# Last down projection with tokens in rows over the transposed residual in PSUM, a norm per token, matmuls of ones at the beginning, and another order of VectorE's work

## The chip, the cores and the metric

One core of one Trainium2 chip runs the whole program. The metric is device time in microseconds (us): the median of three runs of the kernel before is 1358.28 us (1357.35 to 1358.91). A profile of one execution goes with it, and its own time is given below.

## What is computed

Two blocks of two layers each, on 256 tokens of 1024 features, in fp32. Every layer is a mixer (differential attention, neighbourhood attention, convolution and pooling, forgetting and block attention), a feed-forward part of 2816 hidden features, and in the first block a gated extra. Each part reads an RMS norm of the residual `h` and adds to `h`. The end, which the change rewrites, is this:

```python
def rmsnorm_2(x, g):
    xf = x.astype(jnp.float32)
    y = xf * lax.rsqrt(jnp.mean(xf * xf, axis=-1, keepdims=True) + RMS_EPS)
    return (y * g.astype(jnp.float32)).astype(x.dtype)

def conv_ffn(h, w_in, conv_w, conv_b, w_out):
    z = h @ w_in
    u, g = z[..., :D_FF], z[..., D_FF:]
    a = causal_dwconv(u, conv_w) + conv_b
    return (jax.nn.silu(a) * g) @ w_out
...
        h = h + conv_ffn(rmsnorm_2(h, ffn_norm_g[layer]), ffn_w_in[layer],
                         ffn_conv_w[layer], ffn_conv_b[layer], ffn_w_out[layer])
    return rmsnorm_2(h, final_norm_g)
```

## The kernel before

**Layout.** The residual `h` lies in SBUF with features on the partitions: 8 tiles of 128 features by 256 tokens. Every product is made of three fp32r products, since each operand is split in two parts: a weight chunk `raw` of 1 MB is rounded by ScalarE to `whi` (its `split`, L647), VectorE subtracts to get `wlo` (its `split`, L990), and `x`, `hid` and the rest have a high and a low part too. TensorE multiplies high by high, high by low and low by high.

**The ring.** Weights pass through a ring of three chunks (`RING`), in the order of `PLAN`: v, qk, wo, ffn, down, and so on for each layer. SyncE starts the load of chunk c when VectorE has made `wlo` of chunk c-3 (`w_lo`); ScalarE casts it when TensorE is through with chunk c-3 (`w_used`); TensorE starts a chunk at `w_lo`. No scheduler orders anything: each engine's program is written out by hand in the block of that engine, and runs strictly in that order, so an instruction that waits holds back all that stands behind it.

**Attention** (`attention(a)`, a = 0, 1, 2) runs in steps s = 0 to 23, two for each pair of heads j = (s-4)//2. In each step TensorE runs a tile of the qk or wo projection, and between its halves one small product of the attention: scores (L1755), transposes of the probabilities (L1779), probabilities times v (`times_v`, L1795 for a = 0, L1808 else), and for a = 0 transposes of the normalised output (`o_transposes`, L1817). In even steps VectorE adds the bias and takes the maximum (`bias_max`, L1152 or L1158, L1168) and ScalarE takes exponentials (`exps`, L740). In odd steps VectorE normalises (`normalise`, L1185 to L1207), splits a weight chunk, and either scales the output (`norm_o`, L1217, for a = 0; it waits for GpSimd's power L563) or makes its low part (`lo_out`, L1229; `lo_out` of a = 0 is L1225, in even steps). ScalarE copies the transposed probabilities (`take_T`, L753), squares the output (`square_o`, L759) and casts it (`take_o`, L769, L773).

**Norms.** Feature-major `h` makes a norm a chain over all engines: ScalarE squares (L693), GpSimd adds (L499 to L512), TensorE sums over partitions with ones (`sum_squares`, L1524), VectorE adds epsilon (`means`, L1027), GpSimd takes the power -0.5 (L520, five more operations for "mix2", L524 to L529), VectorE builds a diagonal (`diagonals`, L1036), TensorE spreads it (`spread_r`, L1534), VectorE copies it (`take_r`, L1045). Where TensorE does its two parts within other work is set by `SUM_AT` and `SPREAD_AT` for the v projections, and by `middle` for the feed-forward.

**After a wo projection** VectorE adds each pair of feature tiles to `h` (`update`, L1059), ScalarE and VectorE make the next `x` (`take_x` L675, `lo_x` L1016), and VectorE then splits the next two chunks. **Feed-forward** chunks are looped three at a time; VectorE's split of the chunk three ahead stands behind the product of the current chunk with the norm.

**The last stage**: `down(3, "final")` runs 12 chunks (kind "D", 256 output features by 8, 8 or 6 hidden tiles) with the weights stationary: per hidden tile and 128 output features a matmul of 512 columns and one of 256 (`two`, L1546 to L1549). Four times VectorE adds the result to `h` (L1347, L1348), ScalarE squares and scales by gamma (`final_scale`, L878), and after the last pair the whole norm chain follows, then four products (L1504) and four stores (L467) of the feature-major output. The neighbourhood bias `nab` (3 MB) is loaded by GpSimd's queue in two transfers right after the norm of ffn0 (`load_neighbourhood`, L555).

## Time and profile before

| | us |
|---|---|
| median of three runs | 1358.28 |
| the profiled execution's own time | 1354.73 |
| its span, first to last instruction | 1352.7 |
| TensorE busy (matmuls) | 1270.6 |
| VectorE busy | 942.0 |
| ScalarE busy | 678.6 |
| GpSimd busy | 168.9 |
| mean granted TensorE clock | 0.983 |

The profiled execution is 3.6 us shorter than the median. Its time lies 2.0 us over its span. TensorE's clock has two levels in this trace, 1.0 (2.4 GHz) and 0.5 (1.2 GHz). Stages by time: v0 8 to 39 us, attention 0 to 160, ffn0 166 to 299, down0 to 360, gate0 to 390, v1 to 415, attention 1 to 514, ffn1 520 to 648, down1 to 710, gate1 to 740, the input projection "ev" of the convolution and pooling mixer to 798, its output projection "evout" to 824, ffn2 to 956, down2 to 1019, v3 to 1042, attention 2 to 1145, ffn3 to 1277, down3 to 1339, and the end to 1352.7. A matmul row's duration includes its way through the array, so that rows overlap; the pace of a stream is the distance of the starts. fp32 products (both operands fp32) show two records each.

### The profile page before, as it was taken

How to read it: one execution, taken by the hardware profiler on the slowest of the kernel's cores; microseconds unless marked ns; L12 is line 12 of the kernel's file. 1: busy time of each engine (PE TensorE's matmuls, PEld its weight loads, DVE VectorE, ACT ScalarE, POOL GpSimd, SP SyncE). 2: the span in 40 equal slices, each digit the busy share in tenths (PEclk: the TensorE clock that was granted, in tenths of full speed). 3: DMA queues.
4: the chain of work that ended last, by engine and by line, in shares of the span. 5: the costliest groups of instructions: out<-in, count | busy, mean ns of one | idle time of the engine just before them, and what ended most of it. 6: DMA issues, size and time to landing. Idle time of an engine off the chain costs nothing.

```text
span 1352.7 us, 22276 instructions
## 1 busy us (share of the span) xinstructions
PE 1270.6 (94%) x8682; PEld 1158.9 (86%) x8682; DVE 942.0 (70%) x1215; ACT 678.6 (50%) x975; POOL 168.9 (12%) x157
## 2 busy tenths in 40 slices
PE   6987899999999889999999899999999999999996
PEld 5876787888988778888889889999888888999985
DVE  4855668778577665877657794887857765787753
ACT  4544435554455655555445334655435655555541
POOL 3000120016120002000011622000312000100001
PEclk9988899999999999999999999999999999999998
DMA  7422398655646234765564455976465524676550
GB/s 274 147 72 94 94 213 229 186 179 183 201 141 215 94 94 133 218 186 178 181 201 156 150 186 146 271 199 184 150 202 158 162 94 125 177 197 183 174 172 31
DMA packets 286134, 224.22 MB, mean 166 GB/s; under 512 B 8216, under 2 KB 276544, under 8 KB 285936
## 3 DMA queue, kind: packets, MB, share of 16 engines
q1 hardware_dynamic: 283888, 214.25, 52.4%
q0 software_dynamic: 2176, 8.99, 2.5%
q8 instruction: 50, 0.82, 0.3%
q14 instruction: 20, 0.16, 0.0%
HBM read 222.15 MB, written 2.63 MB: 166 GB/s over the span
## 4 chain that ended last, share of the span: by engine, by line
PE 70%; DVE 18%; ACT 5%; issue 3%; DMA 2%; POOL 1%; SPq 0%; POOLq 0%; DVEq 0%; ACTq 0%
PE ps L1548 20%; PE ps L1549 10%; PE ps L1539 10%; PE ps L1540 10%; PE ps L1541 10%; DVE wlo L990 6%; PE ps L1547 2%; DVE x L1016 2%; ACT prob L740 1%; ACT whi L647 1%; PE ps L1755 1%; DMA raw<-in_ffn_w_up 1%; PE ps L1672 1%; DVE nmax L1168 1%; PE ps L1674 1%
## 5 line engine op out<-in xcount | busy, mean ns | idle before, releaser
L990 DVE TENSOR_TENSOR wlo<-raw,whi 128x2048 fp32r<-128x2048 f32 (+1 forms) x206 | 471.8, 2294 | 135.4 <-ACT whi L647 134.4
L647 ACT CAST whi<-raw 128x2048 fp32r<-128x2048 f32 (+1 forms) x206 | 385.2, 1873 | 225.9 <-PE ps L1541 136.6
L1539 PE MATMUL ps<-x,whi 128*128 128x256 f32 (+1 forms) x1640 | 478.5, 292 | 18.5 <-DVE wlo L990 6.4
L1540 PE MATMUL ps<-x,whi 128*128 128x256 f32 (+1 forms) x1640 | 467.7, 285 | 0.0
L1541 PE MATMUL ps<-x,wlo 128*128 128x256 f32 (+1 forms) x1640 | 467.2, 285 | 0.0
L1539 PEld LDWEIGHTS ps<-x,whi 128*128 128x128 f32 (+1 forms) x1640 | 317.7, 194 | 28.5 <-issue 11.2
L1540 PEld LDWEIGHTS ps<-x,whi 128*128 128x128 f32 (+1 forms) x1640 | 318.2, 194 | 0.5
L1541 PEld LDWEIGHTS ps<-x,wlo 128*128 128x128 f32 (+1 forms) x1640 | 317.6, 194 | 0.0
L1548 PE MATMUL ps<-hid,whi 128*128 128x512 f32 x672 | 236.6, 395 | 1.1 <-DVE hid L1274 1.1
L1548 PE MATMUL ps<-x,whi 128*128 128x512 f32 x616 | 222.9, 401 | 8.3 <-DVE wlo L990 8.3
L1549 PE MATMUL ps<-hid,wlo 128*128 128x256 f32 x672 | 188.4, 280 | 0.0
L1549 PE MATMUL ps<-x,wlo 128*128 128x256 f32 x616 | 173.3, 281 | 0.0
L1548 PEld LDWEIGHTS ps<-hid,whi 128*128 128x128 f32 x672 | 126.0, 188 | 29.4 <-DVE hid L1274 1.4
L1548 PEld LDWEIGHTS ps<-x,whi 128*128 128x128 f32 x616 | 116.5, 189 | 34.2 <-DVE wlo L990 6.7
L1549 PEld LDWEIGHTS ps<-hid,wlo 128*128 128x128 f32 x672 | 126.9, 189 | 1.4
L499 POOL TENSOR_TENSOR ssum<-ssum,sq 128x512 f32<-128x512 f32 x24 | 36.2, 1510 | 710.7 <-ACT sq L693 710.7
L1549 PEld LDWEIGHTS ps<-x,wlo 128*128 128x128 f32 x616 | 117.0, 190 | 3.5
L846 ACT COPY gu<-ps 128x512 f32<-128x512 f32 x44 | 25.7, 584 | 85.7 <-PE ps L1547 85.7
L675 ACT ACTIVATE x<-h,gcol 128x256 fp32r<-128x256 f32 x72 | 32.6, 501 | 66.3 <-DVE h L1348 45.7
L740 ACT ACTIVATE prob<-prob,nmax 128x256 f32<-128x256 f32 (+1 forms) x96 | 46.3, 483 | 28.8 <-DVE nmax L1168 25.1
L1016 DVE SCALAR_TENSOR_TENSOR x<-h,gcol,x 128x256 fp32r<-128x256 f32 x72 | 38.7, 580 | 20.9 <-ACT x L675 20.9
L1326 DVE TENSOR_TENSOR gu<-ps,gu 128x512 f32<-128x512 f32 x44 | 30.3, 690 | 27.3 <-ACT gu L846 27.2
(177 smaller groups left out, 1294.2 us busy)
## 6 DMA issues: line engine op xcount, KB each, us to landing
raw<-in_ffn_w_in SPq DMA_DIRECT2D x88, 512.0 KB, 5.1
raw<-in_ffn_w_gate SPq DMA_DIRECT2D x44, 512.0 KB, 4.1
raw<-in_ffn_w_up SPq DMA_DIRECT2D x44, 512.0 KB, 5.2
raw<-in_ffn_w_down SPq DMA_DIRECT2D x32, 512.0 KB, 4.1
raw<-in_ffn_w_out SPq DMA_DIRECT2D x32, 512.0 KB, 4.5
raw<-in_da_w_qkv SPq DMA_DIRECT2D x24, 512.0 KB, 4.6
raw<-in_na_w_qkv SPq DMA_DIRECT2D x24, 512.0 KB, 4.5
raw<-in_od_w_in SPq DMA_DIRECT2D x24, 512.0 KB, 4.6
```

The source lines that it names most:

```text
L499: nc.gpsimd.tensor_tensor(total, total, more, ALU.add).then_inc(add_ok, 1)
L647: nc.scalar.copy(whi[:, c % RING, 0:n], raw[:, c % RING, 0:n]).then_inc(w_hi, 1)
L675: nc.scalar.activation(xs[XBUF[name]][:, k, 0, :], h[:, k, :], ACT.Copy, scale=gamma(name, k)).then_inc(x_hi, 1)
L740: ins = nc.scalar.activation(prob[:, u % 4, off:off + n], prob[:, u % 4, off:off + n], ACT.Exp, bias=nmax[:, u, t:t + 1], accum_out=sums[: ...
L990: nc.vector.tensor_tensor(wlo[:, c % RING, 0:n], raw[:, c % RING, 0:n], whi[:, c % RING, 0:n].bitcast(F32), ALU.subtract).then_inc(w_lo, 1)
L1016: nc.vector.scalar_tensor_tensor(out=x[:, k, 1, :], in0=h[:, k, :], scalar=gamma(name, k), in1=x[:, k, 0, :].bitcast(F32), op0=ALU.mult, o ...
L1326: nc.vector.tensor_tensor(g, ps[:, b0:b0 + 2, 0:S], g, ALU.add).then_inc(sum_ok, 1)
L1539: mm(dst, hi, x[:, 0, :], start=start, stop=False)
L1540: mm(dst, hi, x[:, 1, :], start=False, stop=False)
L1541: return mm(dst, lo, x[:, 0, :], start=False, stop=stop)
L1548: mm(dst, hi, x.rearrange("p a t -> p (a t)"), start=start, stop=False)
L1549: return mm(dst[:, 0:S], lo, x[:, 0, :], start=False, stop=False)
```

## The change

The host now gets the output as tokens by features, and gamma of the last norm goes in as a row of its own. The parts, in the order of the program:

1. TensorE begins with 14 fp32 products of `ones` by `ones` into a bank that is overwritten later.
2. Attention 0: ScalarE's `take_T(j-1)` moves from the odd step into the even step before it, between the two `exps`. VectorE's odd step becomes split, `normalise` twice, `norm_o`.
3. Attention 1 and 2: VectorE's odd step becomes `normalise` twice, `lo_out`, split.
4. `updates`: `update(p+1)` stands ahead of `lo_x(p)`, in wo0, wo1, wo3 and evout.
5. Feed-forward: `spread_r` stands ahead of chunk 2 instead of in its middle.
6. `nab` is loaded in eight pieces of two heads, each after two more chunks of ffn0.
7. `SUM_AT` of v1 moves by 12 matmuls, from (1, 1) to (2, 0).
8. "mix2": the first two chunks of "ev" are gone through in feature tiles 0 to 3, 4 to 5, 6 to 7 instead of 0 to 5, 6 to 7; VectorE splits the chunk `START["ev"] + RING` between `means` and `diagonals`.
9. "ev": `pool_lo` stands ahead of the convolution.
10. down3: 16 fp32 products with the identity put the transposed `h` into banks 0 to 3, and 11 chunks (kind "T", two hidden tiles by 1024 output features) are added to it with `hid` stationary, 24 matmuls of 512 columns each. Bank 2t + n holds tokens 128t and on, features 512n and on. ScalarE squares each bank with a sum per token, VectorE adds epsilon, GpSimd takes the power, VectorE multiplies by gamma and by the power, and SyncE stores four times 256 KB.

```diff
     start, at = {}, 0
     for name, kind, n in plan:
...
 SS = 4
-SUM_AT = {"v0": (2, 0), "v1": (1, 1), "v3": (1, 1)}
+SUM_AT = {"v0": (2, 0), "v1": (2, 0), "v3": (1, 1)}
...
+            for q in (0, 1, 3, 2):
+                if q == 2:
+                    sp.wait_ge(out_ac, 1)
+                else:
+                    sp.wait_ge(out_ok, (1, 2, 0, 3)[q])
+                t, n = q // 2, q % 2
+                sp.dma_start(out[t * P:(t + 1) * P, n * 512:(n + 1) * 512], y_part(q)
+                             ).then_inc(store, 16)
...
+                    for piece in range(HEADS // 2):
+                        gp.wait_ge(w_used, START["ffn0"] + 4 + 2 * piece)
+                        load_neighbourhood(2 * piece)
+                    gp.wait_ge(nab_in, 16 * HEADS)
...
+            gp.wait_ge(w_used, START["ffn3"])
+            gp.dma_start(gfin, w["gfin"].partition_broadcast(P)).then_inc(gfin_in, 16)
+            for t in range(TT):
+                gp.wait_ge(fmean_ok, t + 1)
+                nc.gpsimd.tensor_tensor(final_rstd(t), fsum[:, 4 + t:5 + t], half[:, 0:1], ALU.pow
+                                        ).then_inc(frstd_ok, 1)
...
                             exps(2 * j)
+                        if a == 0 and 0 <= j - 1 < PAIRS:
+                            take_T(j - 1)
+                        if 0 <= j < PAIRS:
                             exps(2 * j + 1)
                     else:
                         if a and 0 <= j - 1 < PAIRS:
                             take_o(j - 1)
                         if a == 0 and 0 <= j - 1 < PAIRS:
-                            take_T(j - 1)
                             square_o(j - 1)
                         if a and 0 <= j < PAIRS:
...
+                for q in range(4):
+                    if q < 3:
+                        ac.wait_ge(part_out, FOURTH["down3"] + q + 1)
+                    else:
+                        ac.wait_ge(w_used, last("down3") + 1)
+                    nc.scalar.activation(fsq(q), bank(q), ACT.Square, scale=D ** -0.5,
+                                         accum_out=fsum[:, q:q + 1]).then_inc(fsq_ok, 1)
+                ac.wait_ge(frstd_ok, 2)
+                ac.wait_ge(fhg_ok, 3)
+                nc.scalar.activation(y_part(2), hg_part(2), ACT.Copy, scale=final_rstd(1)
+                                     ).then_inc(out_ac, 1)
...
+            def updates(wname, banks, name):
+
+                update(wname, banks, name, 0)
+                for p in range(4):
+                    if p < 3:
+                        update(wname, banks, name, p + 1)
+                    lo_x(name, p)
+                split(last(wname) - 1 + RING)
+                split(last(wname) + RING)
...
+                    if a and 0 <= j < PAIRS:
+                        normalise(2 * j)
+                        normalise(2 * j + 1)
+                    if a and 0 <= j - 1 < PAIRS:
+                        lo_out(j - 1)
+                    if 3 <= s < STEPS - 1:
+                        split(START[qk] + s // 2 - 1 + RING)
+                    if a == 0 and 0 <= j < PAIRS:
+                        normalise(2 * j)
+                        normalise(2 * j + 1)
                     if a == 0 and 0 <= j - 1 < PAIRS:
                         norm_o(j - 1)
-                    if a and 0 <= j - 1 < PAIRS:
-                        lo_out(j - 1)
-                    if 0 <= j < PAIRS:
-                        normalise(2 * j)
-                        if a == 0:
-                            normalise(2 * j + 1)
-                    if 3 <= s < STEPS - 1:
-                        split(START[qk] + s // 2 - 1 + RING)
-                    if a and 0 <= j < PAIRS:
-                        normalise(2 * j + 1)
...
             means("mix2")
+            split(START["ev"] + RING)
             diagonals("mix2")
...
             for i in range(6):
                 copy_out(i)
-                split(START["ev"] + i + RING)
+                if i:
+                    split(START["ev"] + i + RING)
                 if i in (1, 2):
                     final_first(4 * (i - 1))
 
+            pool_lo(0)
+            pool_lo(2)
...
             split(START["ev"] + 6 + RING)
-            pool_lo(0)
-            pool_lo(2)
...
+            splits("down3")
+
+            def final_mean(t):
+                ve.wait_ge(fsq_ok, 2 * t + 2)
+                nc.vector.tensor_scalar(fsum[:, 4 + t:5 + t], fsum[:, 2 * t:2 * t + 1],
+                                        fsum[:, 2 * t + 1:2 * t + 2], NORM_EPS, ALU.add, ALU.add
+                                        ).then_inc(fmean_ok, 1)
+
+            def final_gamma(q):
+                ve.wait_ge(fsq_ok, q + 1)
+                n = q % 2
+                nc.vector.tensor_tensor(hg_part(q), bank(q), gfin[:, n * 512:(n + 1) * 512],
+                                        ALU.mult).then_inc(fhg_ok, 1)
+
+            def final_scale(q):
+                ve.wait_ge(frstd_ok, q // 2 + 1)
+                ve.wait_ge(fhg_ok, q + 1)
+                nc.vector.tensor_scalar(y_part(q), hg_part(q), final_rstd(q // 2), None, ALU.mult
                                         ).then_inc(out_ok, 1)
+
+            ve.wait_ge(gfin_in, 16)
+            final_gamma(0)
+            final_mean(0)
+            final_gamma(1)
+            final_scale(0)
+            final_scale(1)
+            final_gamma(2)
+            final_mean(1)
+            final_gamma(3)
+            final_scale(3)
...
                 x = xs[XBUF[name]]
-                for k0, k1 in ((0, 6), (6, KT)):
+                for k0, k1 in ((0, 4), (4, 6), (6, KT)):
...
-                    if first and jj:
-                        middle = lambda: (sum_squares if jj == 1 else spread_r)(name)
+                    if first and jj == 1:
+                        middle = lambda: sum_squares(name)
+                    if first and jj == 2:
+                        spread_r(name)
...
+                    pe.wait_ge(w_lo, c + 1)
+                    pe.wait_ge(hid_lo, 3 * FT + 2 * i + 2)
+
+                    def piece(kk, t, n):
+                        f = 2 * i + kk
+                        ts, cs = slice(t * P, (t + 1) * P), slice(n * 512, (n + 1) * 512)
+                        dst, end = bank(2 * t + n), f == FT - 1
+                        mm(dst, hid[:, f, 0, ts], hi[:, kk, cs], start=False, stop=False)
+                        mm(dst, hid[:, f, 0, ts], lo[:, kk, cs], start=False, stop=False)
+                        return mm(dst, hid[:, f, 1, ts], hi[:, kk, cs], start=False, stop=end)
+
+                    if i < n_chunks - 1:
+                        for kk in range(2):
+                            for t in range(TT):
+                                for n in range(2):
+                                    ins = piece(kk, t, n)
+                        ins.then_inc(w_used, 1)
+                        continue
+                    for t in range(TT):
+                        for n in range(2):
+                            for kk in range(2):
+                                ins = piece(kk, t, n)
+                            ins.then_inc(w_used if t == 1 and n == 1 else part_out, 1)
...
 
+            pe.wait_ge(ones_ok, 1)
+            for _ in range(14):
+                mm(bank(0)[:, 0:P], ones[:], ones[:], start=True, stop=True)
             for layer in range(2):
                 mix, ple, gate = f"mix{layer}", f"ple{layer}", f"gate{layer}"
...
-            down(3, "final")
-            sum_squares("final")
-            spread_r("final")
+            for k in range(KT):
+                for t in range(TT):
+                    mm(bank(2 * t + k // 4)[:, (k % 4) * P:(k % 4 + 1) * P],
+                       h[:, k, t * P:(t + 1) * P], ident, start=k % 4 == 0, stop=False)
+            down_t()
 
```

What this makes of VectorE's order in one pair of heads of attention 0 (L1152/L1190 is `bias_max`, L1217/L1255 `norm_o`, L1225/L1263 `lo_out`, L990/L1018 the split; the first number of each is the line before, the second after). Before:

```order
L1217 TENSOR_SCALAR onrm<-ps,ostat 128x128 x2
L1185 RECIPROCAL rsum<-sums 128x2 x2
L1189 TENSOR_SCALAR rsum<-rsum,tiny 128x2
L1194 TENSOR_SCALAR prob<-prob,rsum 128x256 x2
L1200 SCALAR_TENSOR_TENSOR prob<-prob,rsum 128x256 x2
L990 TENSOR_TENSOR wlo<-raw,whi 128x2048
L1152 SCALAR_TENSOR_TENSOR prob<-dist,ps 128x512
L1168 TENSOR_REDUCE nmax<-prob 128x2
L1152 SCALAR_TENSOR_TENSOR prob<-dist,ps 128x512
L1168 TENSOR_REDUCE nmax<-prob 128x2
L1225 SCALAR_TENSOR_TENSOR x<-ps,col,x 128x256
```

And of the same engine at the same place now:

```order
L1018 TENSOR_TENSOR wlo<-raw,whi 128x2048
L1223 RECIPROCAL rsum<-sums 128x2 x2
L1227 TENSOR_SCALAR rsum<-rsum,tiny 128x2
L1232 TENSOR_SCALAR prob<-prob,rsum 128x256 x2
L1238 SCALAR_TENSOR_TENSOR prob<-prob,rsum 128x256 x2
L1255 TENSOR_SCALAR onrm<-ps,ostat 128x128 x2
L1190 SCALAR_TENSOR_TENSOR prob<-dist,ps 128x512
L1206 TENSOR_REDUCE nmax<-prob 128x2
L1190 SCALAR_TENSOR_TENSOR prob<-dist,ps 128x512
L1206 TENSOR_REDUCE nmax<-prob 128x2
L1263 SCALAR_TENSOR_TENSOR x<-ps,col,x 128x256
```

The split has moved from the end of the odd step to its beginning, and `norm_o` from the beginning to the end.

ScalarE in the same pair of heads, before (L740 `exps`, L753 `take_T`, L759 `square_o`, L769 `take_o`):

```order
L769 ACTIVATE x<-ps,col 128x256
L740 ACTIVATE prob,sums<-prob,nmax 128x256 x4
L753 COPY probT<-ps 128x512
L759 ACTIVATE osq,ostat<-ps 128x128 x2
L728 ACTIVATE qkT<-ps 128x512
L647 CAST whi<-raw 128x2048
```

ScalarE there now:

```order
L796 ACTIVATE x<-ps,col 128x256
L767 ACTIVATE prob,sums<-prob,nmax 128x256 x2
L780 COPY probT<-ps 128x512
L767 ACTIVATE prob,sums<-prob,nmax 128x256 x2
L786 ACTIVATE osq,ostat<-ps 128x128 x2
L755 ACTIVATE qkT<-ps 128x512
L674 CAST whi<-raw 128x2048
```

The copy of the transposed probabilities has moved between the exponentials of the two heads.

VectorE at the norm "mix2", before the change (L1026 and L1027 are `means`, L1036 `diagonals`, L1091 `copy_out`):

```order
L1026 COPY tiny<-ps 128x2
L1027 TENSOR_SCALAR tiny<-ps 128x2
L1036 TENSOR_TENSOR sq<-cst,tiny 128x256 x2
L1409 COPY ya<-ps 128x256
L1410 COPY rst<-ps 128x256
L1091 TENSOR_TENSOR pool<-ps,rst 128x2x256
L990 TENSOR_TENSOR wlo<-raw,whi 128x2048
```

VectorE there now:

```order
L1054 COPY tiny<-ps 128x2
L1055 TENSOR_SCALAR tiny<-ps 128x2
L1018 TENSOR_TENSOR wlo<-raw,whi 128x2048
L1064 TENSOR_TENSOR sq<-cst,tiny 128x256 x2
L1443 COPY ya<-ps 128x256
L1444 COPY rst<-ps 128x256
L1129 TENSOR_TENSOR pool<-ps,rst 128x2x256 x2
```

The split has moved ahead of the diagonals, into the time in which GpSimd works on the powers.

## Rows read from the trace of the kernel before

**Rows 1.** Waits of TensorE: line, waited-for engine and line: total us, times, longest

```profile
PE ps L1795 <- ACT probT L753: 17.4, 7, 3.3
PE ps L1524 <- POOL ssum L512: 9.7, 3, 3.8
PE ps L1779 <- DVE prob L1207: 9.1, 15, 0.9
...
PE ps L1548 <- DVE wlo L990: 8.3, 5, 2.9
PE ps L1539 <- DVE wlo L990: 6.4, 5, 2.6
PE ps L1539 <- DVE x L1016: 3.5, 2, 3.1
...
PE ps L1539 <- DVE x L1417: 2.5, 1, 2.5
...
PE ps L1539 <- DVE x L1225: 2.2, 1, 2.2
```

**Rows 2.** Busy time by stretch: us, then each engine's busy us, granted clock, DMA

```profile
82.04:85.45 3.41, 3.41 (x19) 3.19 (x17) 0.77 (x4) 0.62 (x4) 0.88 (x2) 0.50 0.00 0
93.84:105.95 12.11, 8.76 (x71) 8.05 (x71) 7.73 (x15) 6.14 (x16) 0.88 (x2) 1.00 0.25 87
...
216.00:296.00 80.00, 80.00 (x456) 69.57 (x455) 62.27 (x73) 43.30 (x59) 0.00 (x0) 1.00 0.67 191
```

**Rows 3.** VectorE's timeline in attention 0: start, duration, group, idle before and releaser

```profile
96.75 0.61 DVE L1217 TENSOR_SCALAR onrm<-ps,ostat 128x128 f32<-128x128 f32 x2 [4.17 <-POOL ostat L563]
...
99.38 2.28 DVE L990 TENSOR_TENSOR wlo<-raw,whi 128x2048 fp32r<-128x2048 f32 x1
```

**Rows 4.** ScalarE's timeline in the same pair of heads

```profile
105.33 0.56 ACT L753 COPY probT<-ps 128x512 f32<-128x512 f32 x1
```

**Rows 5.** VectorE's timeline in attention 1

```profile
471.89 0.42 DVE L1229 TENSOR_TENSOR x<-ps,x 128x256 fp32r<-128x256 f32 x1 [1.42 <-ACT x L773]
```

**Rows 6.** TensorE's timeline in ffn0, at two places

```profile
186.65 0.51 PE L1548 MATMUL ps<-x,whi 128*128 128x512 f32 x1 [1.39 <-DVE wlo L990]
...
206.77 0.50 PE L1548 MATMUL ps<-x,whi 128*128 128x512 f32 x1 [2.92 <-DVE wlo L990]
```

**Rows 7.** DMA issues: target and source, queue, count, size of each, us to landing

```profile
nab<-in_rpb POOLq DMA_DIRECT2D x2, 1536.0 KB, 16.9
```

**Rows 8.** GpSimd's timeline: the power at v1, and the first power at "mix2"

```profile
402.69 2.68 POOL L520 TENSOR_TENSOR tiny<-tiny,half 128x2 f32<-128x2 f32 x1 [2.59 <-DVE tiny L1027]
...
757.88 0.70 POOL L524 TENSOR_TENSOR tiny<-tiny,half 128x2 f32<-128x2 f32 x1 [3.47 <-DVE tiny L1027]
```

**Rows 9.** VectorE's timeline at v1: the split beside that power

```profile
402.52 2.28 DVE L990 TENSOR_TENSOR wlo<-raw,whi 128x2048 fp32r<-128x2048 f32 x1
```

**Rows 10.** TensorE's timeline: one `times_v` and what follows; v0; down3's first and last

```profile
93.84 1.16 PE L1795 MATMUL ps<-v,probT 128*128 128x128 f32 x8 [2.16 <-ACT probT L753]
94.76 0.36 PE L1539 MATMUL ps<-x,whi 128*128 128x256 f32 x1
...
17.17 0.39 PE L1672 MATMUL ps<-whi,x 128*128 128x512 f32 x1
...
21.70 0.39 PE L1674 MATMUL ps<-whi,x 128*128 128x512 f32 x1
...
1277.06 0.40 PE L1548 MATMUL ps<-hid,whi 128*128 128x512 f32 x1
...
1338.71 0.40 PE L1547 MATMUL ps<-hid,whi 128*128 128x512 f32 x1
```

**Rows 11.** Timeline of the end, VectorE and SyncE's queue

```profile
1339.15 0.69 DVE L1347 TENSOR_TENSOR h<-ps,h 128x512 f32<-128x512 f32 x1 [9.26 <-PE ps L1547]
...
1347.17 2.50 DVE L1504 TENSOR_TENSOR spare<-spare,rst 128x512 f32<-128x512 f32 x4
1347.88 2.18 SPq L467 DMA_DIRECT2D out<-spare  x4
```

112 lines of the change are left out of this document (46 added, 66 removed).

## The prediction

> **What bounds the kernel now.** I read the page first: TensorE is busy 94% of the span, so time is won only where it waits, where its clock is low, or where it does less. Then the table of what it waits for [rows 1]. Its large lines are each one pattern that comes back: the copy of the transposed probabilities in attention 0 (17.4 us, 7 times), the sums of GpSimd (9.7 us, 3 times), VectorE's normalisation in attention 1 and 2 (9.1 us, 15 times), and weights not yet split (8.3 and 6.4 us). Then the clock. The table by stretches shows 0.5 for 3.41 us after a wait of 2.73 us, with TensorE busy throughout, and 1.00 in an 80 us stretch without a wait [rows 2]; the clock's record has eleven such stretches of 3.41 us besides the start, all beside waits of about 2 us or more, five of them in attention 0. In such a stretch half the work is done, so each costs up to 1.7 us. A wait that goes can thus give back more than itself.
>
> **Attention 0.** A pair of heads takes 12.1 us, in which TensorE is busy 8.8 us and VectorE 7.7 [rows 2]. VectorE first waits 4.17 us for GpSimd's power, then normalises and only then splits, so that the split ends at 101.7 us [rows 3] and delays the maxima, then both exponentials, and behind them the copy `take_T` at 105.33 [rows 4], for which TensorE waits. In the new order the split fills the time of that wait, and `take_T` goes ahead of the second head's exponentials. I worked one pair of odd j through, with TensorE never waiting and its pair beginning at 0: scores end at 1.1, maxima at 3.8, transposes of the pair before at 4.8, `take_T` at 5.4, `times_v` wants it at 6.3. The second exponentials end at 6.6, the split too, `normalise` at 8.8, `norm_o` at 9.6, and TensorE wants that at 11.3. For the next (even) j scores end at 11.3, and `norm_o` at 19.6 where TensorE wants it at 20.1: the slack there is 0.5 us. So TensorE sets the pace, at 8.8 us. That takes all 17.4 us, and of the five low-clock stretches about 1.6 each, 7.9 together: 25.3. VectorE's 7.7 to 8.2 us a pair are near TensorE's 8.8, and GpSimd's powers now fall beside `normalise`; I leave 1.0 for that. At the end of the attention the split no longer stands between `norm_o` and `lo_out`: of the 2.2 us [rows 1] 1.1 go, as the cast and `lo_out` remain; the low-clock stretch behind it goes with an even chance (0.8), and wo0's wait for its second ffn chunk, 0.8, by `updates`. Sum: -25.3 +1.0 -1.1 -0.8 -0.8 = -27.0. The other end is VectorE as the bound with 10.5 us a pair.
>
> **Attention 1 and 2.** `normalise` of the first head waited behind `lo_out`, itself idle 1.42 us for ScalarE's cast [rows 5], though its exponentials were done. Its turn comes 1 us earlier; transposes wait no more, -9.1 [rows 1]. The later `lo_out` and split are wanted only a step or more later.
>
> **updates.** One `update` ahead saves VectorE about 1.7 us on the way to the next x and to its split. The waits for wlo behind wo1 and wo3, 1.8 and 1.7 us, go (both are in [rows 1]'s 8.3 and 6.4). Behind evout ScalarE's cast is late as well; of 2.6 us I take 1.4, and 1.2 for the low clock that follows it now. Sum: -6.1.
>
> **spread_r ahead of chunk 2.** The norm arrives 3 us earlier and the split behind it too. The four waits for it (1.39 us in ffn0 [rows 6], as much in ffn1, 0.58 in ffn2 and ffn3) go: -3.9. VectorE's diagonals are ready 1.2 us before the new place.
>
> **nab in eight pieces.** The two transfers of 1.5 MB took 16.9 us [rows 7] beside the weights, and TensorE waited 2.92 us [rows 6], with a low-clock stretch behind it. A piece is 0.4 MB per two chunks, 12 us, in a ring that has some 7 us to spare. -2.9 -1.6 = -4.5.
>
> **v1.** The 2.23 us before the sums are within the 9.7 [rows 1]. The sums move 12 matmuls later, but VectorE begins `means` only behind a split that ends at 402.5, and GpSimd's power then takes 2.68 us beside the next split [rows 8, 9]. So diagonals are done at 405.8 as before, and TensorE, 2.2 us ahead, waits there. -0.3; the bounds are 0 and -2.2.
>
> **mix2.** The first chunk waited for x of tiles 4 and 5 (3.1 and 0.5 us, the 3.5 of [rows 1]); the second chunk's four tiles now fill that, and the sums come when GpSimd has them, 2.1 us earlier. But the split moves beside GpSimd's chain of six operations. At v1 the same neighbourhood stretched one power to 2.68 us where it takes 0.70 alone [rows 8], with the split running [rows 9]. I take that: the chain ends 2.1 us later than it would, which eats the gain, and TensorE waits some 4 us for the diagonals, long enough for a low clock: +0.8. Without stretching it would be -2.4. The Trainium skill (SBUF — State Buffer, "Who interferes with whom") says that a VectorE instruction with two SBUF inputs and a GpSimd instruction that reads SBUF shut each other out for the whole instruction, the first to issue going first. By that rule the move to this place is a mistake worth the whole 2.1 us; were there no such lock, the total below would be 3.2 us less. The trace agrees with it at v1, and the operand that matters, two SBUF inputs, is that of the split.
>
> **ev.** `pool_lo` moves ahead of work of 8 us that it does not need; its 2.5 us [rows 1] go, and what is put behind it is wanted 3 us or more later. -2.5.
>
> **down3.** Before, 176 pairs of a 512 and a 256 column matmul from 1277.06 to 1339.06, 0.352 us each [rows 10]. Now 264 matmuls of 512 columns with data as stationary side, the form of v0, where 20 take 4.53 us, 0.2265 each [rows 10]: 59.8, or -2.2. The 16 fp32 products with the identity cost what the four of `times_v` do, 0.92 us for four at full clock [rows 10]: +3.7. Nothing hides them, as hid is ready. Sum +1.5. A chunk lasts 5.4 us and needs 1.9 of ScalarE and 2.3 of VectorE: the ring holds. Bounds: 0 and +6.
>
> **The end.** 13.6 us from the last matmul to the span's end [rows 11]. Now: Square of one bank with its sum 0.75 (an estimate: 0.63 for the Square of 512 columns now and 0.1 for reading the sum), mean 0.2, power 0.75, scale 0.6: the last operand is ready 2.5 us after the last matmul, the second store is issued at about 3.3, and the end lay 2.6 us behind the last issue: 5.8. The other three banks are done by then or beside it. -7.8, between -7.0 and -9.0.
>
> **The beginning.** 14 fp32 products at low clock end near 7 us, before the first weights at 8.4, so they delay nothing. The first 12 matmuls then run at full clock, 2.4 us sooner, but TensorE must wait until 25.7 for GpSimd's sums (3.6 us now, in [rows 1]), 1.3 us longer, and the low clock that follows that wait costs as much or more: +0.5, between -1.6 and +1.7.
>
> **The sum.** -27.0 -9.1 -6.1 -3.9 -4.5 -0.3 +0.8 -2.5 +1.5 -7.8 +0.5 = -58.4 us. From the profiled execution's 1354.7 that is 1296.3; it was 3.6 us below the median, so I take the same off the median: 1358.3 - 58.4 = 1299.9 us.
>
> **The rivals.** (a) VectorE binds attention 0. With 8.2 us of own work, links between dependent steps and locks against GpSimd, a pair takes 10.5 instead of 8.8. For it speaks the slack of 0.5 us; against it, that VectorE's order has idle time only once per two pairs and still fits. Seven pairs by 1.7: 1311.8 us. (b) The freed waits turn up as waits for weights: with denser work the ring's load, cast and split are late in attention 0 and in down3. For it speaks that wlo is the second releaser now; against it, 191 GB/s in the 80 us without a wait [rows 2], more than down3 needs. At 1 us for each of 11 chunks, 1310.9. (c) Better: mix2 is not stretched, v1 and evout give their whole waits, no low clock after attention 0: 1299.9 - 3.2 - 1.9 - 1.2 - 0.8 = 1292.8. (d) The change does not do what it says: attention 0 keeps its waits because another copy or power comes last; only the rest comes, 1299.9 + 25 = 1325. (e) Slower: a clock that denser work does not keep. All of some 1260 us of matmul work would have to run at a mean of 0.955 instead of nearly 1 to eat 58 us; at 0.93 it is 1299.9 + 95 = 1395. Against it: 1.00 over the 80 us without any wait [rows 2].
>
> **How the numbers follow.** Forecast, 1296 to 1306: 0.53. (c) 0.14. (a) 0.13. (b) 0.09. (d) 0.09. (e) 0.01, and 0.01 for something unseen. The range takes the forecast, (c), (a) and (b): 1290 to 1317. A difference of 0.2%, 2.7 us, is what can be told from no change: faster 0.98, same 0.01, slower 0.01.
>
> **What would show it.** In the changed profile, the row of `times_v` waiting for probT should be gone or under 3 us, pairs 8.8 us apart, and no low clock between 66 and 150 us. L1779's waits gone; no wait of 2.9 us in ffn0; GpSimd's first power at mix2 near 2.7 us instead of 0.70, and a new wait for the diagonals there of about 4 us; one of 2 us at v1's diagonals. Down3 from ffn3's end to the last matmul 63.5 us; the end 5.8 us. I am wrong if pairs of attention 0 take over 10 us, or down3 over 66.

## The result and the profile after

The changed kernel takes 1296.0 us (median of four runs, 1295.85 to 1298.22), beside 1358.6 us (1357.35 to 1359.62) for the kernel before: a ratio of 0.9543, 95% interval 0.9527 to 0.956. The forecast was 1299.9 us, with a range of 1290 to 1317, and 58.4 us less than before; the medians lie 62.6 us apart, the two profiled executions 56.3 (spans of 1352.7 and 1296.4). The second is a difference of two single executions: that of before was 3.9 us below its median, that of after 2.2 above. On three other chips the kernel before had medians of 1355.4 to 1356.1, and the changed one, run again, 1296.64, which is 59 us apart. So the sum was about right in size, but it was right by terms that missed in both directions, as the comparison by stage shows.

What TensorE waits for in the changed kernel, to be read beside [rows 1] (line, engine and line waited for, total us, times, longest):

```profile
PE ps L1590 <- DVE wlo L1018: 5.4, 4, 1.7
PE ps L1575 <- POOL ssum L531: 5.0, 2, 4.5
PE ps L1723 <- DVE wlo L1025: 2.9, 1, 2.9
PE ps L1599 <- DVE wlo L1018: 2.6, 2, 1.3
PE ps L1585 <- DVE sq L1064: 2.5, 1, 2.5
PE ps L1575 <- DVE wlo L1018: 1.9, 1, 1.9
```

The 17.4 us for the transposed probabilities and VectorE's 9.1 us of the normalisation are gone. Two rows stand for new waits: `spread_r` at mix2 waits 2.5 us for the diagonals (L1585, 0.86 us before), and v1's sums wait 1.9 us for weights (L1575, where 2.23 us for GpSimd's sums stood). The second ffn chunk waits 1.3 us at each of its four places (in L1590 and L1599), where 0.80, 1.79, 2.58 and 1.69 us stood at wo0, wo1, evout and wo3. The 4.5 us of L1575 are v0's sums, 3.62 us before.

Busy time by stretch (us from:to, length, then the busy us of TensorE, its weight loads, VectorE, ScalarE and GpSimd with counts, the granted clock, DMA share and GB/s), to be read beside [rows 2]:

```profile
93.43:101.97 8.54, 8.54 (x73) 8.03 (x72) 8.33 (x16) 6.25 (x18) 0.92 (x2) 1.00 0.35 125
25.12:31.95 6.83, 5.56 (x15) 4.62 (x16) 2.81 (x3) 2.66 (x2) 4.12 (x5) 0.50 0.41 134
56.00:132.00 76.00, 73.60 (x601) 68.77 (x599) 63.67 (x121) 49.26 (x128) 7.59 (x16) 1.00 0.46 141
369.86:373.27 3.41, 3.41 (x10) 2.74 (x10) 2.36 (x3) 0.89 (x1) 2.72 (x2) 0.50 0.75 247
721.43:724.84 3.41, 3.41 (x14) 3.06 (x14) 1.70 (x4) 0.00 (x0) 1.53 (x3) 0.50 1.00 326
```

One pair of heads of attention 0 (first row) takes 8.54 us instead of 12.11, with TensorE busy in all of it. The clock is full through the attention (third row). It is low in three places only, besides the start and the last microseconds: around the sums of v0 (from 25.12 us, within the wait for them), behind the sums of v1, and behind the new wait at mix2.

Where the 56.3 us come from, by stage. Each length is the distance between the first records of two events that both traces have (a norm's sums, its `spread_r`, the first product with hid; for the end of ffn3 of the changed kernel the first product with the identity):

| stretch | before | after | difference | forecast |
|---|---|---|---|---|
| start to `spread_r` of v0 | 33.31 | 34.99 | +1.7 | +0.5 |
| to ffn0's sums (attention 0) | 142.48 | 113.86 | -28.6 | -27.0 |
| to the end of ffn0 | 122.78 | 116.42 | -6.4 | -5.9 |
| down0, gate0, v1 to its `spread_r` | 107.67 | 109.16 | +1.5 | -0.3 |
| attention 1 to ffn1's sums | 123.87 | 116.52 | -7.4 | with attention 2: -12.6 |
| ffn1 | 118.14 | 116.41 | -1.7 | -1.4 |
| down1, gate1 to its `spread_r` | 73.62 | 73.39 | -0.2 | 0 |
| ev, evout to ffn2's sums | 114.72 | 111.02 | -3.7 | -4.3 |
| ffn2 | 119.78 | 119.23 | -0.6 | -0.6 |
| down2, v3 | 76.87 | 77.32 | +0.5 | 0 |
| attention 2 to ffn3's sums | 124.05 | 120.27 | -3.8 | see above |
| ffn3 | 119.77 | 118.94 | -0.8 | -0.6 |
| down3 and the end | 75.68 | 68.90 | -6.8 | -6.3 |

(The forecast's terms are put where they fall; `updates` is split over the stretches of its four places.)

The lengths before are those of one execution. Other traces below have the same code in some of these stretches, and two stretches scatter widely: attention 0 takes 142.5, 140.3 and 141.3 us in the three traces that have its old code, and ffn0 takes 120.8 to 124.3 us in six. Measured against these, attention 0 gains 26.4 to 28.6 us and not one sharp number.

The last stage, to be read beside [rows 10] and [rows 11] (timeline: start, duration, engine, line, group, idle before and releaser):

```profile
1227.53 3.74 PE L2024 MATMUL ps<-cst,h 128*128 128x128 f32 x32
1231.02 0.47 PE L1803 MATMUL ps<-whi,hid 128*128 128x512 f32 x1
...
1290.61 3.54 SPq L486 DMA_DIRECT2D out<-spare  x4
1290.76 0.39 PE L1805 MATMUL ps<-whi,hid 128*128 128x512 f32 x1
...
1291.18 0.60 ACT L902 ACTIVATE spare<-ps 128x512 f32<-128x512 f32 x1 [0.67 <-PE ps L1805]
1291.68 0.19 ACT L902 ACTIVATION_READ_ACCUMULATOR spare<-ps 128x1 f32 x1
...
1292.20 0.55 POOL L652 TENSOR_TENSOR fsum<-fsum,half 128x1 f32<-128x1 f32 x1 [2.13 <-DVE fsum L1531]
1292.79 0.72 ACT L906 ACTIVATE spare<-spare,fsum 128x512 f32<-128x512 f32 x1 [0.91 <-POOL fsum L652]
```

The 16 products with the identity (two records each) take 3.5 us until the first real one, where 3.7 were forecast. The last matmul starts at 1290.76, and from its end at 1291.15 the chain Square, sum, mean, power, scale, store takes 5.3 us to the end of the span, where 5.8 were forecast and 13.6 were needed before.

### The profile page after: what moved, and what is told of

Its sections match the earlier page's. It is cut to its first block, busy times and chain, and to the rows that moved or that the text cites. A ratio compares the mean times of both kernels' runs of the same rounds, so it can differ in the third digit from the quotient of the medians.

```text
span 1296.4 us, 22210 instructions
## 1 busy us (share of the span) xinstructions
PE 1260.0 (97%) x8648; PEld 1149.5 (89%) x8648; DVE 943.4 (73%) x1208; ACT 675.2 (52%) x971; POOL 170.3 (13%) x168
## 4 chain that ended last, share of the span: by engine, by line
PE 84%; DVE 9%; ACT 2%; DMA 2%; issue 1%; POOL 1%; SPq 1%; POOLq 0%; ACTq 0%
PE ps L1599 19%; PE ps L1590 13%; PE ps L1591 12%; PE ps L1592 12%; PE ps L1600 10%; DVE wlo L1018 3%; DVE x L1044 3%; PE ps L1598 2%; PE ps L1838 2%; ACT whi L674 2%; PE ps L1803 1%; PE ps L1805 1%; PE ps L1804 1%; PE ps L1862 1%; PE ps L1723 1%; PE ps L1891 1%
## 5 line engine op out<-in xcount | busy, mean ns | idle before, releaser
L1018 DVE TENSOR_TENSOR wlo<-raw,whi 128x2048 fp32r<-128x2048 f32 (+1 forms) x205 | 467.9, 2286 | 134.9 <-ACT whi L674 134.0
L1590 PE MATMUL ps<-x,whi 128*128 128x256 f32 (+1 forms) x1640 | 474.7, 289 | 11.2 <-DVE wlo L1018 5.4
L1590 PEld LDWEIGHTS ps<-x,whi 128*128 128x128 f32 (+1 forms) x1640 | 313.8, 191 | 21.3 <-issue 9.3
L1591 PEld LDWEIGHTS ps<-x,whi 128*128 128x128 f32 (+1 forms) x1640 | 314.1, 192 | 0.5
L1592 PEld LDWEIGHTS ps<-x,wlo 128*128 128x128 f32 (+1 forms) x1640 | 313.8, 191 | 0.0
L1599 PE MATMUL ps<-x,whi 128*128 128x512 f32 x616 | 222.2, 399 | 2.6 <-DVE wlo L1018 2.6
L1599 PE MATMUL ps<-hid,whi 128*128 128x512 f32 x504 | 177.7, 395 | 1.1 <-DVE hid L1312 1.1
L1600 PE MATMUL ps<-hid,wlo 128*128 128x256 f32 x504 | 141.3, 280 | 0.0
L1599 PEld LDWEIGHTS ps<-x,whi 128*128 128x128 f32 x616 | 115.9, 188 | 28.4 <-issue 3.2
L1599 PEld LDWEIGHTS ps<-hid,whi 128*128 128x128 f32 x504 | 94.5, 188 | 22.5 <-DVE hid L1312 1.4
L518 POOL TENSOR_TENSOR ssum<-ssum,sq 128x512 f32<-128x512 f32 x22 | 34.2, 1558 | 524.4 <-ACT sq L720 523.9
L1600 PEld LDWEIGHTS ps<-hid,wlo 128*128 128x128 f32 x504 | 95.2, 189 | 1.0
L1044 DVE SCALAR_TENSOR_TENSOR x<-h,gcol,x 128x256 fp32r<-128x256 f32 x72 | 48.1, 714 | 11.1 <-ACT x L702 11.1
L1364 DVE TENSOR_TENSOR gu<-ps,gu 128x512 f32<-128x512 f32 x44 | 30.4, 691 | 30.5 <-ACT gu L875 30.4
```

The lines of the kernel that those rows point to most:

```text
L518: nc.gpsimd.tensor_tensor(total, total, more, ALU.add).then_inc(add_ok, 1)
L1018: nc.vector.tensor_tensor(wlo[:, c % RING, 0:n], raw[:, c % RING, 0:n], whi[:, c % RING, 0:n].bitcast(F32), ALU.subtract).then_inc(w_lo, 1)
L1044: nc.vector.scalar_tensor_tensor(out=x[:, k, 1, :], in0=h[:, k, :], scalar=gamma(name, k), in1=x[:, k, 0, :].bitcast(F32), op0=ALU.mult, o ...
L1364: nc.vector.tensor_tensor(g, ps[:, b0:b0 + 2, 0:S], g, ALU.add).then_inc(sum_ok, 1)
L1590: mm(dst, hi, x[:, 0, :], start=start, stop=False)
L1591: mm(dst, hi, x[:, 1, :], start=False, stop=False)
```

## The experiments

There were twelve more runs: eleven other kernels, and the changed kernel again. They come from three chips, so each median is given with its ratio to the kernel before on the same chip, and the stage lengths of the traces are used where less than 2 us is at stake. Most stages that the code leaves alone come out within 0.1 us of each other between traces. Where a low clock falls in one and not in the other, or a load comes later, they differ by up to 3.5 us, so a stage length says little unless the clock in it is compared too.

### Attention 0: which of the two edits

Both edits alone, upon the kernel before:

```diff
                             exps(2 * j)
+                        if a == 0 and 0 <= j - 1 < PAIRS:
+                            take_T(j - 1)
+                        if 0 <= j < PAIRS:
                             exps(2 * j + 1)
...
                         if a == 0 and 0 <= j - 1 < PAIRS:
-                            take_T(j - 1)
                             square_o(j - 1)
...
-                    if a == 0 and 0 <= j - 1 < PAIRS:
-                        norm_o(j - 1)
+                    if a == 0 and 3 <= s < STEPS - 1:
+                        split(START[qk] + s // 2 - 1 + RING)
                     if a and 0 <= j - 1 < PAIRS:
                         lo_out(j - 1)
                     if 0 <= j < PAIRS:
                         normalise(2 * j)
                         if a == 0:
                             normalise(2 * j + 1)
-                    if 3 <= s < STEPS - 1:
+                    if a == 0 and 0 <= j - 1 < PAIRS:
+                        norm_o(j - 1)
+                    if a and 3 <= s < STEPS - 1:
                         split(START[qk] + s // 2 - 1 + RING)
```

> The kernel before with two edits of attention 0 alone: take_T between the exponentials of the two heads, and VectorE's odd step in the order split, normalise twice, norm_o. Theory: this is the largest part of the whole gain, -26 to -28 us against before (the sum had -25.3 +1.0 -1.1 -0.8 for it), that is about 1331. The waits of TensorE for probT are gone, pairs stand 8.5 to 8.8 us apart, no stretch at clock 0.5 between 66 and 150 us. Rival: part of the 28.3 us by which the end of attention 0 moved in the changed kernel came from elsewhere (the beginning, or what comes before it); then -22 or less.

Measured: 1327.92 us, ratio 0.9798 (0.9772 to 0.9824), which is 27.4 us. From v0's `spread_r` to ffn0's sums 113.67 us instead of 142.48: -28.8 (-26.6 and -27.6 against the two other traces with the old code), and the changed kernel takes 113.86. The whole gain of that stretch is these two edits.

VectorE's part alone (the last hunk):

> The kernel before with VectorE's order of attention 0 alone (split, normalise twice, norm_o in the odd step), take_T left behind both exponentials. Theory: the late split is the cause of most of the wait, so this gives -19 to -24 us, and a short wait for probT of about 0.5 to 1 us per pair remains. Rival: the copy's place behind the second exponentials is the cause; then this gives -8 us or less and waits of over 1.5 us remain.

Measured: 1333.22 us, ratio 0.9832 (0.9809 to 0.9856), -22.8; the stretch -23.9.

ScalarE's part alone (the first two hunks):

> The kernel before with take_T alone moved between the exponentials of the two heads, VectorE's order left. Theory (the late split is the cause): the copy comes 1.2 us earlier in each pair, the pair goes from 12.1 to about 11, -8 to -10 us. Rival (the copy's place is the cause): -20 us or more. Third case: the two edits are each enough, and both single kernels come within 5 us of the kernel with both.

Measured: 1347.74 us, ratio 0.9938 (0.9913 to 0.9963), -8.4; the stretch -12.1.

The waits of TensorE ahead of `times_v` (its line is L1797 in both) in these two, first the one with VectorE's order, then the one with `take_T` moved:

```profile
PE ps L1797 <- ACT probT L753: 3.1, 4, 0.8
```

```profile
PE ps L1797 <- DVE x L1227: 11.5, 7, 2.3
```

So VectorE's order is the main cause, as the prediction has it. That edit moves two things, the split to the front and `norm_o`, with its wait for GpSimd's power, to the end; no run moves only one, so how much of the gain is the split's and how much `norm_o`'s is not shown. With the new order, the copy behind both exponentials still costs 0.74 us in every second pair (pairs of 8.64 and 9.4 us in turn, one of 10.3); with only the copy moved, every pair takes 10.96 us, since the maxima still stand behind the split (the second row names `lo_out`, which follows the same maxima and ends 0.1 us after the copy). The two gains add to 36 us, more than the 28.8 that both give, so they are in part gains on the same wait. The pace with both is 8.5 us (once 9.4), TensorE's own.

### Is a low clock worth 1.6 us by itself?

The sum took 17.4 us of waits and 7.9 for five stretches of low clock. This kernel leaves the waits and tries to keep the clock up:

```diff
                         if s % 2 == 1 and 0 <= j - 1 < PAIRS:
+                            if s < 16:
+                                for _ in range(6):
+                                    mm(bank(3)[:, 0:P], ones[:], ones[:], start=True, stop=True)
                             times_v(j - 1)
```

> The kernel before with work added for the clock alone: in attention 0, in odd steps before step 16, six fp32 products of ones (about 1.4 us at full clock) into a free bank right ahead of times_v, inside the time in which TensorE waits for probT. They add nothing to the result. The waits that remain are near 1 us. Theory A: the low-clock stretches lie in the path (scores and transposes run in them), but TensorE has 3 us to spare in each pair, so clearing them gives 0 to -3 us. Theory B, the one of the sum: each stretch that goes gives 1.6 us by itself, -6.4 us for four. If the clock stays at 0.5 after such a wait all the same, nothing comes of it: 0 to +2.

Measured: 1358.13 us, ratio 1.0012 (0.9996 to 1.0029): nothing won. The trace shows why:

```profile
PE ps L1795 <- ACT probT L753: 12.3, 7, 3.3
```

```profile
76.78 1.50 PE L1832 MATMUL ps<-ones 128*128 128x128 f32 x12
80.33 0.99 PE L1795 MATMUL ps<-v,probT 128*128 128x128 f32 x6 [2.05 <-ACT probT L753]
```

```profile
81.08:84.49 3.41, 3.41 (x18) 3.19 (x18) 0.92 (x5) 0.76 (x5) 0.88 (x2) 0.50 0.00 0
```

The six products cut the waits but leave up to 2 us of each, and behind these the clock fell all the same at two of the four places, in pairs of 12.37 and 12.90 us. Where it did not fall, the pair took 12.10 to 12.14 us. In the kernel before the pairs with a low stretch take 13.04, 13.02, 12.49 and 12.45 us and those without 12.10 and 12.11. So as long as VectorE and ScalarE set the pace, those four cost 2.6 us and not 6.4. Theory A holds. The test is a weak one, since it did not clear all stretches; the distances of the pairs say it better than its total.

What a stretch costs there follows from where it begins. Over the twelve that begin in such pairs in the traces of before, of this kernel and of the two below that keep attention 0 as it was, the pair takes 13.0 us when the stretch begins within 0.1 us of `times_v`, 12.8 to 12.9 at 0.2 us behind it, 12.4 to 12.5 at 0.6 to 0.8 us, and 12.1, as with none, at 1.1 us. One of the last kind, from the run of the last stage alone, whole pair at a mean clock of 0.86:

```profile
90.52:102.63 12.11, 10.25 (x71) 9.54 (x71) 7.73 (x15) 6.14 (x16) 0.88 (x2) 0.86 0.25 88
```

That fits the prediction's working, in which the scores, for which VectorE waits, end 1.1 us behind the pair's beginning; it was not tested by itself. That the sum came out right all the same is bookkeeping: once no wait is left, TensorE gets back both its idle time and the half speed, and only both together are the gain (17.4 us of waits, six stretches at up to 1.7 and 1.1 us at the end make 28.7).

### The beginning

```diff
-            pe.wait_ge(ones_ok, 1)
-            for _ in range(14):
-                mm(bank(0)[:, 0:P], ones[:], ones[:], start=True, stop=True)
```

taken out of the changed kernel.

> The changed kernel without the 14 fp32 products of ones at the beginning. Theory: they bring the full clock 9 us earlier, but TensorE then waits for GpSimd's sums 4.55 us instead of 3.62, and a longer low clock (6.8 us instead of 3.4) follows, so they gain nothing: without them the same time within 0.5 us, or up to 1.7 us less. Rival: they help by the 2.4 us that the first matmuls are sooner; then 1 to 2.4 us more without them.

Measured: 1296.18 us, ratio 0.956 (0.9539 to 0.9581), against 0.9567 of the changed kernel run again (below); the intervals overlap. In six traces with the products `spread_r` of v0 stands at 32.9 to 35.0 us, in this one at 33.1, and in the traces of the kernel before and of the six built upon it, all without them, at 30.5 to 34.5. The scatter is that of the first loads. The products of ones give nothing that can be told here, and cost nothing that can be told.

### mix2: the split beside GpSimd's powers

```diff
             means("mix2")
-            split(START["ev"] + RING)
             diagonals("mix2")
...
-                if i:
-                    split(START["ev"] + i + RING)
+                split(START["ev"] + i + RING)
```

> The changed kernel with one part undone: at the norm of mix2, the split of the fourth ev chunk stands again behind the diagonals and the first copy_out, the tiles' order (0 to 3, 4 to 5, 6 to 7) is left as changed. Theory (the split beside GpSimd's powers stretches one of them from 0.70 to 2.68 us): GpSimd's first power is back at about 0.7 us, the wait for the diagonals of 2.5 us and the 3.4 us of low clock behind it shrink, -2 to -3 us. Rival: the split is then late in its new place and TensorE waits for wlo instead, so that nothing is won: within 1 us of the changed kernel, with a wait for wlo of 1.5 us or more at the fourth chunk.

Measured: 1295.45 us, ratio 0.9556 (0.9535 to 0.9576). GpSimd's first power and TensorE's `spread_r` in the changed kernel:

```profile
715.72 2.68 POOL L543 TENSOR_TENSOR tiny<-tiny,half 128x2 f32<-128x2 f32 x1 [2.36 <-DVE tiny L1055]
...
721.19 1.87 PE L1585 MATMUL ps<-sq,ones 128*128 128x256 f32 x4 [2.50 <-DVE sq L1064]
```

and with the split put back, GpSimd's power and what TensorE waits for later:

```profile
714.74 0.70 POOL L543 TENSOR_TENSOR tiny<-tiny,half 128x2 f32<-128x2 f32 x1 [2.37 <-DVE tiny L1055]
...
723.71 0.35 PE L1588 MATMUL ps<-x,whi 128*128 128x256 f32 x1 [0.99 <-DVE wlo L1018]
```

The power goes from 2.68 to 0.70 us, and the wait of 2.5 us for the diagonals is gone: the stretching is the split's doing. But the split is then late for its own chunk, 0.99 us. From mix2's sums to the end of ffn2 the kernel takes 196.51 us; four traces whose code is that of the changed kernel there take 196.7 to 197.8, the spread being that of low clocks, so 0.2 to 1.2 us come back and not 2 to 3. Each theory had a part of it: the stretching is real, and the old place has a price too. Part of what is won at mix2 is also lost later: this trace waits 0.78 us for weights in the middle of ffn2, where the changed kernel's first trace has no wait.

### v1: the place of the sums

```diff
-SUM_AT = {"v0": (2, 0), "v1": (2, 0), "v3": (1, 1)}
+SUM_AT = {"v0": (2, 0), "v1": (1, 1), "v3": (1, 1)}
```

> The changed kernel with the place of v1's sums put back from (2, 0) to (1, 1), 12 matmuls earlier. Theory: the move made v1 slower, since TensorE now waits 1.9 us for the weights of chunk 2 ahead of the sums, the norm comes later, and low clock follows; with the old place v1 takes 25.2 us again instead of 26.5, -1.3 us. Rival: the wait for chunk 2 comes from gate1 and stands at any place of the sums; then within 0.4 us.

Measured: 1294.49 us, ratio 0.9556 (0.9534 to 0.9578). From gate0's `spread_r` to v1's, 34.28 us instead of 35.54: -1.3, the expected number. But a low clock lies behind the sums in the one trace and none in the other, and that is not the code's doing. With full clock the new place takes 34.80 us (the changed kernel again, below) and the old one 34.28; with a low stretch the new one takes 35.54 to 35.56 (four traces) and the old one 35.86 to 35.92 (four traces of the table at the end). So the move costs 0.5 us at full clock and gains 0.3 at low clock, and most of the 1.3 us is the clock. The sums and VectorE at v1, in the changed kernel:

```profile
369.54 0.74 PE L1575 MATMUL ps<-ones,ssum 128*128 128x1 f32 x4 [1.88 <-DVE wlo L1018]
...
367.19 2.29 DVE L1018 TENSOR_TENSOR wlo<-raw,whi 128x2048 fp32r<-128x2048 f32 x1 [1.83 <-ACT whi L674]
370.31 0.16 DVE L1055 TENSOR_SCALAR tiny<-ps 128x2 f32<-128x2 f32 x1 [0.83 <-PE ps L1575]
370.39 2.28 DVE L1018 TENSOR_TENSOR wlo<-raw,whi 128x2048 fp32r<-128x2048 f32 x1
```

and with the old place:

```profile
364.90 0.58 PE L1575 MATMUL ps<-ones,ssum 128*128 128x1 f32 x4 [2.24 <-POOL ssum L531]
...
364.90 2.29 DVE L1018 TENSOR_TENSOR wlo<-raw,whi 128x2048 fp32r<-128x2048 f32 x1 [1.82 <-ACT whi L674]
367.11 0.15 DVE L1055 TENSOR_SCALAR tiny<-ps 128x2 f32<-128x2 f32 x1
```

At (2, 0) the sums stand behind the wait for chunk 2, and what TensorE waits for there is the `wlo` that VectorE makes just ahead of `means`. So the sums can't start before the split ends, and `means` comes 0.83 us after it instead of at once. This much is the place's doing.

### The order of `updates`

```diff
-                update(wname, banks, name, 0)
                 for p in range(4):
-                    if p < 3:
-                        update(wname, banks, name, p + 1)
+                    update(wname, banks, name, p)
                     lo_x(name, p)
```

> The changed kernel with one part undone: update(p) and lo_x(p) in turn again, instead of one update ahead, in wo0, wo1, wo3 and evout. Theory (the order helps nothing, since lo_x now falls beside GpSimd's additions and two lo_x take 1.9 instead of 0.9 us): the wait for wlo at the second ffn chunk, 1.3 us in all four places now, becomes 0.8, 1.8, 2.6 and 1.7 as before, +1.6 us in all with a low clock more, at most +3; and two lo_x take 0.9 us. Rival (the prediction's): the order is worth 6.1 us, so +6. Third: it costs, -1 or less.

Measured: 1296.59 us, ratio 0.9569 (0.9547 to 0.9591). The stretches of the four places are 1.5 us longer in sum (about -0.1, +1.4, +0.4 and -0.1 for wo0, wo1, evout and wo3). VectorE, GpSimd and TensorE behind wo1 in the changed kernel (L1087 is `update`, L1044 `lo_x`, L518 to L531 the adding of squares):

```profile
479.67 1.91 DVE L1044 SCALAR_TENSOR_TENSOR x<-h,gcol,x 128x256 fp32r<-128x256 f32 x2
481.51 0.68 DVE L1087 TENSOR_TENSOR h<-ps,h 128x512 f32<-128x512 f32 x1
482.11 3.58 DVE L1044 SCALAR_TENSOR_TENSOR x<-h,gcol,x 128x256 fp32r<-128x256 f32 x4
485.62 4.48 DVE L1018 TENSOR_TENSOR wlo<-raw,whi 128x2048 fp32r<-128x2048 f32 x2
...
479.88 2.86 POOL L518 TENSOR_TENSOR ssum<-ssum,sq 128x512 f32<-128x512 f32 x2 [106.09 <-ACT sq L720]
...
488.04 0.47 PE L1599 MATMUL ps<-x,whi 128*128 128x512 f32 x1 [1.32 <-DVE wlo L1018]
```

and in turn again:

```profile
479.66 0.89 DVE L1044 SCALAR_TENSOR_TENSOR x<-h,gcol,x 128x256 fp32r<-128x256 f32 x2 [0.58 <-ACT x L702]
...
483.01 5.57 DVE L1018 TENSOR_TENSOR wlo<-raw,whi 128x2048 fp32r<-128x2048 f32 x2
...
478.57 1.28 POOL L518 TENSOR_TENSOR ssum<-ssum,sq 128x512 f32<-128x512 f32 x1 [106.69 <-ACT sq L720]
...
485.98 0.47 PE L1597 MATMUL ps<-x,whi 128*128 128x512 f32 x1 [1.79 <-DVE wlo L1018]
```

The new order does fill VectorE's waits of 0.58 us for ScalarE. But now two `lo_x` run beside GpSimd's additions and take 1.91 us instead of 0.89, and four take 3.58. In turn, it is the two splits behind them that run beside an addition, and take 5.57 us instead of 4.48. Counted from v1's `spread_r` (374.43 and 372.53 us), VectorE begins the splits at 111.2 us in the new order and at 110.5 in the old, and TensorE is released by the first at 113.6 and 113.45. So the new order doesn't release TensorE earlier, but 0.16 us later, and 0.12 and 0.13 us later behind wo0 and wo3. The wait is 1.32 instead of 1.79 us only because TensorE reaches it 0.6 us later.

The 1.4 us at wo1 are a low clock. In the run above a stretch of 3.41 us at 0.5 begins at 487.41 us, 1.4 us behind the wait of 1.79; in seven traces with the old order, before and the six built upon it, the clock stays full behind the same wait:

```profile
487.41:490.82 3.41, 3.41 (x15) 3.02 (x13) 1.16 (x1) 0.57 (x1) 0.00 (x0) 0.50 1.08 296
```

Behind evout the wait is 1.32 instead of 2.58 us, and a low clock followed the long one in six of eight traces and the short one in none of six, so there the order may be worth something; mix2's low clocks stand in the way of a number. The prediction's rival of 6 us falls. The first theory's reason holds, that the stretched operations eat the gain, but its 1.6 us are not shown: what these traces show for the order lies between nothing and 1.5 us.

### The new last stage alone

All hunks of the last stage upon the kernel before, nothing else.

> The kernel before with the new last stage alone: the transposed residual in PSUM, 11 chunks with tokens in rows, the norm per token and the row-major output; all else as before. Theory: this part is worth what the sum gave it, +1.5 in down3 and -7.8 at the end, -6.3 us; from the changed kernel's trace, +1.6 and -8.3, -6.7. Down3 from ffn3's last product to its last matmul takes 63.6 us, the end behind it 5.3. Rival: in the changed kernel the stage profited from the order of the rest; alone it has waits for weights, and comes to -4 or less.

Measured: 1348.76 us, ratio 0.9952 (0.9933 to 0.9971), -6.5. From ffn3's `spread_r` to the end of the span 182.49 us instead of 189.26: -6.8. Its products with the identity begin at 1273.56 and its last matmul at 1336.79, 63.2 us (with that matmul 63.6), and the end takes 5.3. The part is worth the same alone as with the rest, where the stage gives -6.8 too.

```profile
1273.56 3.74 PE L2014 MATMUL ps<-cst,h 128*128 128x128 f32 x32
...
1336.79 0.39 PE L1798 MATMUL ps<-whi,hid 128*128 128x512 f32 x1
```

### The neighbourhood bias in pieces alone

```diff
-                    load_neighbourhood()
-                    gp.wait_ge(nab_in, 16 * 2)
+                    for piece in range(HEADS // 2):
+                        gp.wait_ge(w_used, START["ffn0"] + 4 + 2 * piece)
+                        load_neighbourhood(2 * piece)
+                    gp.wait_ge(nab_in, 16 * HEADS)
```

> The kernel before with the neighbourhood bias loaded in eight pieces, and nothing else. Theory: the two large transfers cause the wait of 2.92 us in ffn0 and the low clock behind it; in pieces both go, -4.5 us (2.9 and 1.6), and ffn0 takes 112 us or less from its sums on. Rival: the wait comes from the weights' own load, late in any case behind wo0; then 1.5 us or more of it stays, and the gain is under 2 us.

Measured: 1352.71 us, ratio 0.9977 (0.996 to 0.9994), -3.1. Ffn0 takes 118.12 us from its sums on instead of 122.78: -4.65 (my 112 us in the expectation left out the 6 us between sums and `spread_r`). The five other traces with ffn0's old code take 120.83 to 124.29 us there, with waits of 2.52 to 4.49 us and none to 6.8 us of low clock behind them, so the part gives 2.7 to 6.2 us, by what the clock does. The only wait left there is the one of 1.39 us behind `spread_r`:

```profile
186.62 0.50 PE L1551 MATMUL ps<-x,whi 128*128 128x512 f32 x1 [1.39 <-DVE wlo L993]
```

A piece lands in 5.9 us, where a half of the whole took 16.9 [rows 7]. The interval of the ratio, 0.8 to 5.4 us, holds the stage's 4.65. The two profiled executions differ by 2.8 us only, since a low clock fell at v1 in this one (+1.6) and not in the one before.

### A version with two places mended, and the changed kernel again

```diff
-SUM_AT = {"v0": (2, 0), "v1": (2, 0), "v3": (1, 1)}
+SUM_AT = {"v0": (2, 0), "v1": (1, 1), "v3": (1, 1)}
...
             means("mix2")
-            split(START["ev"] + RING)
             diagonals("mix2")
+            split(START["ev"] + RING)
```

> The changed kernel with two places mended: v1's sums back at (1, 1), and at mix2 the split of the fourth ev chunk right behind the diagonals, ahead of the first copy_out, where GpSimd's powers are over. Theory: v1 takes 25.2 us instead of 26.5; at mix2 GpSimd's first power takes 0.7 us, the wait of 2.5 us for the diagonals goes, and no wait for wlo of 1 us comes in its place, as the split is some 2 us earlier than behind copy_out. Together -1.3 and -2.0 to -3.0, so 1292 to 1293. Rival: the split there delays ScalarE's or VectorE's copies and the wait comes back at another chunk; then -1.3 to -2 in all.

> The changed kernel once more, on the same chip as the version above, to have both side by side and a second trace. Theory: places that show low clock behind a wait of about 2 us in one execution show none in another of the same code (v0's norm, v1, mix2), each worth up to 1.7 us, while all other stages take the same time within 0.1 us; median 1296 within 1 us. Rival: the low clock is the same each time, and the difference of single executions lies in the loads.

Measured: the mended version 1296.01 us (1293.0 to 1296.38), ratio 0.9553 (0.9538 to 0.9569); the changed kernel 1296.64 us (1296.27 to 1299.05), ratio 0.9567 (0.9551 to 0.9582). The ratios differ by 1.9 us and their intervals overlap, so the totals don't tell the two apart. By the traces v1's part is -1.25 us against the first trace and -0.5 against the second, both with full clock there, and from mix2's sums to the end of ffn2 it takes 195.26 us against the 196.7 to 197.8 of the four traces with the changed kernel's order there (197.59 in both of the changed kernel itself), -1.4 to -2.5. At mix2, VectorE and GpSimd:

```profile
716.18 2.29 DVE L1018 TENSOR_TENSOR wlo<-raw,whi 128x2048 fp32r<-128x2048 f32 x1
...
712.83 0.70 POOL L543 TENSOR_TENSOR tiny<-tiny,half 128x2 f32<-128x2 f32 x1 [2.36 <-DVE tiny L1055]
```

The power is short, no wait for diagonals is left, and none for wlo came in its place at mix2; one of 0.51 us came in the middle of ffn2, so the rival had a small part. The split wants to be behind the diagonals and ahead of the copies. I would take this version, for its places and not for a proven total.

The changed kernel's second trace has the same stages within 0.1 us but for three: the start (-1.3), v1 (-0.7) and the stretch from mix2 to ffn2's sums (-1.6). The last is given back whole in ffn2, where a wait for weights comes that the first trace doesn't have:

```profile
822.55 0.39 PE L1590 MATMUL ps<-x,whi 128*128 128x256 f32 x1 [1.60 <-DVE wlo L1018]
```

The split that it waits for stands behind a cast for which ScalarE sat idle 6.73 us until the chunk's load had landed. So what is won ahead of ffn2 can be lost to the weights' load there, which is the prediction's rival (b) in a place where it was not looked for. The first theory holds in part. Only at v1 has one trace a low clock and the other none; at v0 and mix2 both have one, at another moment. The differences stay under 1.7 us, but ffn2's, with its wait, was not foreseen.

## Why the prediction was right, and where its steps were not

**Attention 0** was sized at -26.2 without wo0's update and gave -28.8 (its two edits alone, against the profiled execution of before; -26.6 and -27.6 against the other two traces with the old code, so that part of the difference is which execution was profiled). The reasons held: the wait for probT gone, pairs of 8.5 us (8.8 forecast), no low clock between 66 and 150 us. Against the profiled execution the difference is the three guesses around them: the 1.0 us left for VectorE's nearness and locks was not needed, the low clock behind the attention, taken at half, went whole, and each of the five stretches is 1.7 us and not 1.6. These make 1.0 + 0.8 + 0.5 of the 2.6. The clock's record has ten stretches of 3.41 us and not the eleven that the prediction counts: its eleventh is a longer one that begins at 1341.6 us, in the end. That the split held up the maxima is the prediction's reason; the runs show it for split and `norm_o` together. Rival (a), a pair of 10.5 us by VectorE, is dead: it is busy 8.33 of 8.54 us and still never late, though near. TensorE's wait for `lo_out` behind the attention went from 2.2 us [rows 1] to 1.08, the forecast 1.1 less.

**Attention 1 and 2**: -9.1 forecast. The updates' share taken out with the kernel that undoes them, they gave -6.4 and -3.9, in sum -10.3, or -11.4 without the low clock at wo1 in that trace (1.1 us of it lie in the stretch). Of 15 waits one of 0.6 us is left. Where the gain beyond 9.1 comes from is not shown; no low clock lies in these stretches before.

**updates** is the step that failed: "one `update` ahead saves VectorE about 1.7 us on the way to the next x", -6.1 in all. Measured: 1.5 us over the four places at most, of which 1.4 is a low clock at wo1. The saving never reaches the split: VectorE begins it 0.7 us later than in the old order, since two `lo_x` go from 0.89 to 1.91 us once they meet GpSimd's additions. That needs no more than the reason that I used at mix2, and I didn't apply it here. The Trainium skill (SBUF — State Buffer, "Who interferes with whom") lets a VectorE instruction with two SBUF inputs and a GpSimd instruction that reads SBUF shut each other out. The trace agrees: `lo_x` reads h and x from SBUF, and GpSimd's two additions, from 479.88 to 482.74 us, lie over the two `lo_x` of 479.67 to 481.58.

**spread_r and nab**: -3.9 and -4.5 forecast. nab alone gave -4.65 (2.7 to 6.2 by the clock of the trace beside it). Ffn0's rest (1.7), ffn1 (1.7), ffn2 (0.6) and ffn3 (0.8) give 4.8 us, in which the updates have a small part. Both steps right in kind, and in size as far as that scatter tells.

**v1**: -0.3 forecast, +1.3 measured against the profiled execution, outside the bounds of 0 and -2.2 that I gave. Of this 0.5 is the place (both at full clock), still outside, and the rest the low clock, which fell in one trace and not in the other. The failed sentence is that VectorE "begins `means` only behind a split that ends at 402.5". True, but I took the sums to be ready by then, "12 matmuls later". The moved sums stand behind TensorE's wait for that very split, so TensorE waits for VectorE's split, and then VectorE 0.83 us for TensorE's sums. I bounded below by the rows and forgot that a matmul moved past a wait takes the wait on.

**mix2**: the mechanism was as told. The power took the forecast 2.68 us, and TensorE waited for the diagonals with a low clock behind, but 2.5 us where 4 were forecast; three shorter waits stand before it, 0.7, 0.4 and 1.1 us. Together with `pool_lo` and evout the stretch came to -3.7 against -4.3. That undoing the split's place gives only 1.1 us says that the -2.4 that the prediction has without stretching was too good: the old place has a wait of 1 us of its own.

**down3 and the end**: +1.5 and -7.8, sum -6.3. Measured -6.8, alone and with the rest. The end took 5.3 instead of 5.8 (the prediction's four terms add to 2.3 and not 2.5, and its 3.3 and 2.6 to 5.9; the last scale ended 2.4 us behind the last matmul); down3 63.6 against 63.5.

**The beginning**: +0.5 forecast, +1.7 in this pair of traces, at the edge of its bounds, and not distinguishable from zero over fourteen traces.

**The sum.** -58.4 forecast, and -56.3 in the profiled pair. Better than forecast in this pair: attention 0 by 2.6 us, attention 1 and 2 by 1.2, nab with `spread_r` by about 1, the last stage by 0.5. Worse: updates by 4.6, v1 by 1.6, the start by 1.2. (With the low clock at wo1 taken out, attention 1 and 2 gain some 1.1 us more and updates gives about nothing.) The total came out closer than its terms because errors of both signs met. That is luck: updates was wrong by at least 4.6 of its 6.1 us, and the terms that made up for it had been sized too low.

## What to carry to other kernels

Where one engine's strict order makes a chain late, look first for an instruction that could run during a wait already in that order: giving VectorE a 2.28 us split and the normalisation to do in its 4.17 us wait gave 23.9 of the 28.8 us. When you fill such a gap on VectorE with an operation that reads two SBUF operands, look at what GpSimd does there at that moment, each time and not only once. And when a matmul is moved past a wait, ask who makes what is waited for: if it is the engine that needs the matmul's result, it will wait in its turn. Last, before a stage's difference is put down to an edit, look whether the clock was the same in both traces.

## What the runs showed of the hardware

Whether the clock falls behind a wait is not the same in each execution of the same code. The sums of v1 wait 2.23 or 2.24 us in seven traces whose code is the same there:

| kernel | wait | clock behind it | sums to `spread_r` |
|---|---|---|---|
| before | 2.23 | full | 5.99 |
| both edits of attention 0 | 2.24 | full | 5.99 |
| VectorE's order alone | 2.23 | 0.5 for 3.41 us | 7.58 |
| `take_T` alone | 2.24 | 0.5 for 3.41 us | 7.62 |
| products of ones in the waits | 2.24 | 0.5 for 3.41 us | 7.64 |
| nab in pieces | 2.23 | 0.5 for 3.41 us | 7.59 |
| the last stage alone | 2.23 | full | 6.03 |

Two of these in the records, that of nab in pieces and that of before, both from 1.19 us behind the start of the sums (stretch, length, busy times and granted clock):

```profile
396.75:400.16 3.41, 3.41 (x9) 2.64 (x8) 3.38 (x3) 0.60 (x1) 2.15 (x1) 0.50 0.31 79
```

```profile
401.44:404.85 3.41, 3.41 (x16) 2.82 (x15) 3.36 (x3) 1.67 (x2) 2.17 (x1) 1.00 0.31 77
```

Nine matmul records lie in one and sixteen in the other. The same varies at the start: in these seven traces, which begin with the same code, 7 to 13 matmul records stand ahead of the first full clock. The Trainium skill (TensorE: Matmul & The Clock Gate, Part 1) calls the number of slow matmuls at a kernel's start run-variable. These traces agree, and show the same in the middle of a kernel. Such differences, 1.6 us at v1, go with what separates executions of one kernel: of 14 of the kernel before on one chip the shortest, 1351.52 us, has a mean clock of 0.986 and the longest, 1360.00, of 0.978. So a part worth under 2 us has to be read from stage lengths, between traces that have the same clock there. And a low clock costs by where it falls. At mix2 the same 3.41 us make ffn2's sums 1.5 us later behind the last wait than ahead of it, since the wait of 2.50 us for the diagonals was then only 1.03 (of these 1.5 us, 0.7 in the trace shown and all in the changed kernel's second were lost again in ffn2):

```profile
717.88 1.13 PE L1585 MATMUL ps<-sq,ones 128*128 128x256 f32 x4 [1.03 <-DVE sq L1064]
```

That row is from the kernel with v1's sums put back; its low clock stood from 712.2 to 715.6 us.
